# A 512-token Fourier mix inside a two-block kernel: one fold over tokens against two mirror folds with half the frequencies

## The reference, cut to what matters

```python
FOURIER_GROUPS, FOURIER_GROUP_DIM = 4, 128

def fourier_mix(f, w_f):          # f: (1, 512, 512)
    b, l, _ = f.shape
    fg = f.reshape(b, l, FOURIER_GROUPS, FOURIER_GROUP_DIM).astype(jnp.float32)
    z = jnp.fft.fft2(fg, axes=(1, 3), norm='ortho').real
    return z.reshape(b, l, FOURIER_WIDTH).astype(f.dtype) @ w_f

def merge_branches(h, ret_d, four_d, w_bg, b_bg, w_out):
    gates = jax.nn.sigmoid(h @ w_bg + b_bg)
    g_r, g_f = jnp.split(gates, N_BRANCHES, axis=-1)
    return (g_r * ret_d + g_f * four_d) @ w_out
```

## Time and profile before

| | us |
|---|---|
| median of 3 runs | 1664.74 |
| lowest and highest | 1662.05, 1671.71 |
| the profiled execution | 1659.04 |
| its span, first to last instruction | 1657.3 |
| mean granted TensorE clock, share of full | 0.983 |
| six steps with Fourier products, within the span | 1093.3 to 1146.8 |

### The profile page before, as it was taken

The page is one execution under the profiler, slowest core; times in us unless marked ns, Lnnn a source line. Parts: engine busy times, 40 slices in busy tenths (PEclk is TensorE's granted clock), DMA queues, the critical chain, the costliest instruction groups (busy, mean ns, idle before and its releaser), DMA issues.

```text
span 1657.3 us, 19932 instructions
## 1 busy us (share of the span) xinstructions
PE 1587.4 (96%) x7623; PEld 1273.9 (77%) x7623; DVE 895.6 (54%) x1071; ACT 772.0 (47%) x909; POOL 122.1 (7%) x95
## 2 busy tenths in 40 slices
PE   6999999999979899989799999999999999999998
PEld 5777777788867678878588888888887788888886
DVE  6424334345468788977453452523365655565464
ACT  5554445322457788855444333443124443443343
POOL 1101001000024233300010000000000000000000
PEclk9999999999979999999899999999999999999999
DMA  5457563234259999842412121321431333233222
GB/s 148 140 168 244 176 210 127 77 101 136 98 204 366 344 363 357 296 147 77 143 53 77 60 66 51 105 77 51 152 102 51 102 99 102 79 101 101 82 78 70
DMA packets 184033, 231.33 MB, mean 140 GB/s; under 512 B 14939, under 2 KB 155543, under 8 KB 180639
## 3 DMA queue, kind: packets, MB, share of 16 engines
q1 hardware_dynamic: 176223, 217.84, 39.9%
q0 software_dynamic: 7744, 12.60, 2.1%
HBM read 227.76 MB, written 18.37 MB: 149 GB/s over the span
## 4 chain that ended last, share of the span: by engine, by line
PE 85%; DMA 4%; DVE 4%; ACT 3%; issue 2%; SPq 1%; POOL 0%; ACTq 0%; POOLq 0%; DVEq 0%
PE psum L452 21%; PE psum L454 20%; PE psum L453 20%; DMA hg<-h_rows,at_row 3%; PE psum L1815 2%; PE psum L1816 2%; PE psum L1817 2%; PE psum L752 1%; PE psum L1791 1%; PE psum L834 1%; DMA vec<-in_ret_decay_b 1%; PE psum L1842 1%; DVE pre L531 1%; PE psum L1239 1%; PE psum L1843 1%
## 5 line engine op out<-in xcount | busy, mean ns | idle before, releaser
L452 PE MATMUL psum<-h_hi,w_hi 128*128 128x512 f32 x1160 | 462.9, 399 | 7.7 <-DVE w_lo L429 3.3
L454 PE MATMUL psum<-h_hi,w_lo 128*128 128x512 f32 x1160 | 453.1, 391 | 0.0
L453 PE MATMUL psum<-h_lo,w_hi 128*128 128x512 f32 x1160 | 453.0, 390 | 0.0
L429 DVE TENSOR_TENSOR w_lo<-raw,w_hi 128x2048 fp32r<-128x2048 f32 (+2 forms) x99 | 223.6, 2259 | 239.7 <-ACT w_hi L425 239.7
L452 PEld LDWEIGHTS psum<-h_hi,w_hi 128*128 128x128 f32 x1160 | 218.4, 188 | 67.7 <-issue 16.2
L454 PEld LDWEIGHTS psum<-h_hi,w_lo 128*128 128x128 f32 x1160 | 218.3, 188 | 46.9
L453 PEld LDWEIGHTS psum<-h_lo,w_hi 128*128 128x128 f32 x1160 | 218.6, 188 | 44.2 <-issue 1.4
L425 ACT ACTIVATE w_hi<-raw 128x2048 fp32r<-128x2048 f32 (+2 forms) x100 | 187.9, 1879 | 76.5 <-PE psum L454 68.8
L482 ACT ACTIVATE sq<-x 128x512 f32<-128x512 f32 x56 | 35.3, 632 | 151.8 <-DVE x L1352 105.2
L1761 DVE TENSOR_TENSOR w_lo_more<-raw_more,w_hi_more 128x2048 fp32r<-128x2048 f32 x34 | 77.8, 2287 | 20.3 <-ACT w_hi_more L1754 19.9
L1761 DVE TENSOR_TENSOR w_lo<-raw,w_hi 128x2048 fp32r<-128x2048 f32 x34 | 77.8, 2287 | 12.1 <-ACT w_hi L1754 11.7
(11 more groups left out here) (388 smaller groups left out, 2594.3 us busy)
## 6 DMA issues: line engine op xcount, KB each, us to landing
raw<-in_w_up SPq DMA_DIRECT2D x67, 512.0 KB, 8.2
wm_raw<-in_w_mod SPq DMA_DIRECT2D x24, 1024.0 KB, 5.5
raw<-in_w_in SPq DMA_DIRECT2D x18, 1024.0 KB
raw<-in_w_in SPq DMA_DIRECT2D x33, 512.0 KB
raw_more<-in_w_down SPq DMA_DIRECT2D x24, 512.0 KB, 5.4
raw<-in_w_gate SPq DMA_DIRECT2D x23, 512.0 KB, 5.4
raw_more<-in_w_gate SPq DMA_DIRECT2D x22, 512.0 KB, 5.3
raw_more<-in_w_up SPq DMA_DIRECT2D x22, 512.0 KB, 7.7
```

Of the source, the lines that this page charges most:

```text
L429: dve.tensor_tensor(w_lo[j][:, 0:tiles, :], raw[j][:, 0:tiles, :], w_hi[j][:, 0:tiles, :].bitcast(F32), ALU.subtract).then_inc(G["lo_ready ...
L452: pe.matmul(to, w_hi[j][:, tile, :], hi_k, start=(k == 0), stop=False)
L453: pe.matmul(to, w_hi[j][:, tile, :], lo_k, start=False, stop=False)
L454: return pe.matmul(to, w_lo[j][:, tile, :], hi_k, start=False, stop=last)
```

## The change

The token fold becomes a fold at two levels. Token t is paired with 512 - t: differences go to tokens 257 to 511, sums stay at 1 to 255; tokens 0 and 256 pair with themselves. Then sums are paired again around 128, and differences around 384. VectorE reads one operand of each pair backwards. Six instructions per group take the place of two. After this the four kinds of output (even and odd frequencies, cosine and sine part) each depend on one slice of 128 tokens, with one token left over (column 128 of the row).

Over features there are four products of 128 columns, cosines for the sums and sines for the differences, and one with a single column of weights, the left-over token, which goes to partition 0 of a second bank. ScalarE copies 512 columns and, in a second instruction, 128 columns of one partition. Over tokens there are five products: 129 columns that contract over one partition (the left-over token), then 129, 128, 127 and 128 columns, into one bank. Frequencies 0 to 256 come out as a cosine and a sine part.

ScalarE copies the sine part to `z_sin`; VectorE (`unfold`) writes two columns as they are and makes the others as sum and, for the mirrored frequencies, difference, with rows written in steps of 2 and -2, into `pre`. ScalarE waits for that and rounds `pre` into `z_hi`; VectorE makes `z_lo` from `pre`, now behind `yr_lo`. The table `dft_l` shrinks from 2048 to 641 columns per partition; the memory layout behind it is kept by padding.

```diff
--- before.py
+++ after.py
@@ -129,9 +129,11 @@
     j = np.arange(P)
     a = 2 * np.pi * np.outer(j, j) / P
     dft_d = np.concatenate([np.cos(a), -np.sin(a)], axis=1).astype(np.float32) / np.float32(256)
-    to = np.concatenate([t[0::2], t[1::2]])
-    a = 2 * np.pi * (np.outer(t[:T // 2], to) % T) / T
-    dft_l = np.stack([np.cos(a), np.sin(a)]).astype(np.float32)
+    j = np.arange(P + 1)
+    wave = lambda f, of, to: f(2 * np.pi * (np.outer(of, to) % T) / T)
+    dft_l = np.concatenate([wave(np.cos, j[:P], 2 * j), wave(np.cos, 127 - j[:P], 2 * j[:P] + 1),
+                            wave(np.sin, j[:P], 2 * j[1:P]), wave(np.sin, 128 - j[:P], 2 * j[:P] + 1),
+                            np.tile((-1.0) ** j, (P, 1))], axis=1).astype(np.float32)
     col, part = np.arange(P)[None, :], np.arange(P)[:, None]
     at = np.arange(1)[None, :]
 
@@ -379,7 +381,9 @@
                 yr_hi = buffers(r)("yr_hi", [P, KC, T], F32R)
             sb = buffers(s)
             z_room = sb("z_room", [P, NT * T])
-            dft_l = sb("dft_l", [P, 2, NT // 2, T])
+            dft_l = sb("dft_l", [P, T + P + 1])
+            z_sin = sb("z_sin", [P, 2, 2 * P])
+            z_pad = sb("z_pad", [P, 2 * T - P - 1])
             dft_d = sb("dft_d", [P, 2 * P])
             z_gap = sb("z_gap", [P, 1536])
             z_hi = sb("z_hi", [P, 4, T], F32R)
@@ -2545,8 +2549,7 @@
             sp.wait_ge(H["t_decayed"], 32)
             sp.wait_ge(H["t_vtok"], 8)
             sp.dma_start(dft_d[:, :], const["dft_d"]).then_inc(Z["z_const"], 16)
-            sp.dma_start(dft_l[:, :, :, :], const["dft_l"].rearrange("a (i p) t -> p a i t", p=P))\
-              .then_inc(Z["z_const"], 16)
+            sp.dma_start(dft_l[:, :], const["dft_l"]).then_inc(Z["z_const"], 16)
             for s in range(4):
                 load_slot(sp, G_GF + s, (G_GF + s) % 2, pairs(a["w_branch_gate_2"], D + s * 2 * P))
             for s in range(4):
@@ -2557,8 +2560,10 @@
                 load_slot(sp, G_FO + s, (G_FO + s) % 2,
                           [(0, 16, T, a["w_four_out_2"][:, s * T:(s + 1) * T].rearrange("(k p) n -> p k n", p=P))])
 
-        def in_order(g):
-            return psum[:, 5 + g % 2, :].rearrange("p (o j) -> p j o", o=2)
+        EVEN_C, ODD_C, EVEN_S, ODD_S, END = 0, P + 1, 2 * P + 1, 3 * P, 4 * P
+
+        def folded(g):
+            return fd[:, g, :, :].rearrange("p i n -> p (i n)")
 
         def four_tensor(pe):
             rest = ret_after_tensor(pe, 3)
@@ -2569,11 +2574,12 @@
                     pe.wait_ge(H["t_state"], 56)
                 else:
                     pe.wait_ge(Z["z_copied"], g)
-                pe.wait_ge(Z["z_fold"], 2 * g + 2)
-                for i in range(NT):
-                    done = pe.matmul(psum[:, SA + i // 2, (i % 2) * 256:(i % 2) * 256 + 256],
-                                     f_t[:, g, i * P:(i + 1) * P], dft_d[:, :], start=True, stop=True)
-                done.then_inc(Z["z_d"], 1)
+                pe.wait_ge(Z["z_fold"], 6 * g + 6)
+                for i, (t0, part) in enumerate(((0, 0), (P + 1, 0), (2 * P, 1), (3 * P, 1))):
+                    pe.matmul(psum[:, SA, i * P:(i + 1) * P], f_t[:, g, t0:t0 + P], dft_d[:, part * P:(part + 1) * P],
+                              start=True, stop=True)
+                pe.matmul(psum[0:1, SB, 0:P], f_t[:, g, P:P + 1], dft_d[:, 0:P], start=True, stop=True)\
+                  .then_inc(Z["z_d"], 1)
 
             def over_tokens(g):
                 pe.wait_ge(Z["z_copied"], g + 1)
@@ -2581,12 +2587,10 @@
                     pe.wait_ge(H["t_y"], 9)
                 if g >= 2:
                     pe.wait_ge(Z["z_lo"], g - 1)
-                for odd in range(2):
-                    cols = slice(odd * 2 * P, odd * 2 * P + 2 * P)
-                    for n in range(4):
-                        i, part = n // 2, n % 2
-                        done = pe.matmul(psum[:, 5 + g % 2, cols], fd[:, g, 2 * odd + i, part * P:(part + 1) * P],
-                                         dft_l[:, part, i, cols], start=(n == 0), stop=(n == 3))
+                to, of = psum[:, 5 + g % 2, :], folded(g)
+                pe.matmul(to[:, EVEN_C:ODD_C], of[0:1, 4 * P:5 * P], dft_l[0:1, END:END + P + 1], start=True, stop=False)
+                for i, (c0, c1) in enumerate(((EVEN_C, ODD_C), (ODD_C, EVEN_S), (EVEN_S, ODD_S), (ODD_S, END))):
+                    done = pe.matmul(to[:, c0:c1], of[:, i * P:(i + 1) * P], dft_l[:, c0:c1], start=(i > 0), stop=True)
                 done.then_inc(Z["z_l"], 1)
 
             for t in range(12):
@@ -2643,15 +2647,16 @@
                     rest[t]()
                 if 5 <= t < 9:
                     act.wait_ge(Z["z_d"], t - 4)
-                    act.activation(fd[:, t - 5, :, :], psum[:, SA:SA + 2, :].rearrange("p b (i n) -> p (b i) n", n=256),
-                                   ACT.Copy).then_inc(Z["z_copied"], 1)
+                    act.activation(folded(t - 5)[:, 0:4 * P], psum[:, SA, :], ACT.Copy)
+                    act.activation(folded(t - 5)[0:1, 4 * P:5 * P], psum[0:1, SB, 0:P], ACT.Copy).then_inc(Z["z_copied"], 1)
                 if t >= 5:
                     four_gate(act, t - 5)
                 if 7 <= t < 11:
                     g = t - 7
                     act.wait_ge(Z["z_l"], g + 1)
-                    act.activation(z_hi[:, g, :].rearrange("p (j o) -> p j o", o=2), in_order(g), ACT.Copy)\
-                       .then_inc(Z["z_hi"], 1)
+                    act.activation(z_sin[:, g % 2, 1:], psum[:, 5 + g % 2, EVEN_S:END], ACT.Copy).then_inc(Z["z_hi"], 1)
+                    act.wait_ge(Z["z_fold"], 6 * 4 + g + 1)
+                    act.activation(z_hi[:, g, :], pre[:, g % 2, :], ACT.Copy).then_inc(Z["z_hi"], 1)
                 if t >= 8:
                     gated_hi(t - 8)
             four_gate(act, 7)
@@ -2680,12 +2685,33 @@
                    .then_inc(Z["z_ylo"], 1)
 
             def fold(g):
-                early, late = f_t[:, g, 0:2 * P], f_t[:, g, 2 * P:4 * P]
+                n = 6 * g
+
+                f = f_t[:, g, :]
+                mirrored = ((f[:, 255:0:-1], f[:, 257:512]),
+                            (f[:, 127::-1], f[:, 129:257]),
+                            (f[:, 511:384:-1], f[:, 257:384]))
                 dve.wait_ge(Z["z_f"], g + 1)
-                dve.tensor_tensor(late, early, late, ALU.subtract).then_inc(Z["z_fold"], 1)
-                dve.wait_ge(Z["z_fold"], 2 * g + 1)
-                dve.scalar_tensor_tensor(out=early, in0=early, scalar=2.0, in1=late, op0=ALU.mult, op1=ALU.subtract)\
-                   .then_inc(Z["z_fold"], 1)
+                for level in (mirrored[:1], mirrored[1:]):
+                    for near, far in level:
+                        dve.tensor_tensor(far, near, far, ALU.subtract).then_inc(Z["z_fold"], 1)
+                    n += len(level)
+                    dve.wait_ge(Z["z_fold"], n)
+                    for near, far in level:
+                        dve.scalar_tensor_tensor(out=near, in0=near, scalar=2.0, in1=far, op0=ALU.mult, op1=ALU.subtract)\
+                           .then_inc(Z["z_fold"], 1)
+                    n += len(level)
+                    dve.wait_ge(Z["z_fold"], n)
+
+            def unfold(g):
+                dve.wait_ge(Z["z_hi"], 2 * g + 1)
+                at, z = psum[:, 5 + g % 2, :], pre[:, g % 2, :]
+                even_c, odd_c, even_s, odd_s = at[:, 1:P], at[:, ODD_C:EVEN_S], z_sin[:, g % 2, 1:P], z_sin[:, g % 2, P:]
+                dve.tensor_copy(z[:, 0:2 * P + 1:2 * P], at[:, 0:P + 1:P])
+                dve.tensor_tensor(z[:, 2:2 * P:2], even_c, even_s, ALU.add)
+                dve.tensor_tensor(z[:, T - 2:2 * P:-2], even_c, even_s, ALU.subtract)
+                dve.tensor_tensor(z[:, 1:2 * P:2], odd_c, odd_s, ALU.add)
+                dve.tensor_tensor(z[:, T - 1:2 * P:-2], odd_c, odd_s, ALU.subtract).then_inc(Z["z_fold"], 1)
 
             for t in range(12):
                 if t % 2 == 0:
@@ -2695,13 +2721,14 @@
                 if 2 <= t < 6:
                     fold(t - 2)
                 if 7 <= t < 11:
-                    g = t - 7
-                    dve.wait_ge(Z["z_hi"], g + 1)
-                    dve.tensor_tensor(z_lo[:, g, :].rearrange("p (j o) -> p j o", o=2), in_order(g),
-                                      z_hi[:, g, :].bitcast(F32).rearrange("p (j o) -> p j o", o=2), ALU.subtract)\
-                       .then_inc(Z["z_lo"], 1)
+                    unfold(t - 7)
                 if t >= 8:
                     gated_lo(t - 8)
+                if 7 <= t < 11:
+                    g = t - 7
+                    dve.wait_ge(Z["z_hi"], 2 * g + 2)
+                    dve.tensor_tensor(z_lo[:, g, :], pre[:, g % 2, :], z_hi[:, g, :].bitcast(F32), ALU.subtract)\
+                       .then_inc(Z["z_lo"], 1)
             for c in range(4, KC):
                 gated_lo(c)
             for c in range(KC):
```

## The result

The changed kernel took 1655.84 us (median of 16 runs, 1648.94 at the least), the kernel before 1663.88 (16 runs). One execution of each kernel was far slower than all others (1982.46 and 1788.88 us) and is left out of the ratio. The ratio of the means of the other 15 is 0.9942 with a 95% interval of [0.9925, 0.9958]: 9.6 us less, 0.58%. The forecast was 10.5 us less.

What follows compares the result with a forecast made beforehand. TensorE's queue was taken as the bound: 20.7 - 9.0 - 1.2 = 10.5 us off the profiled 1659.04 gives 1648.5, or 1654.2 against the median of 1664.74. The range was 1648 to 1660 us.

Steps and rivals of the forecast that it cites:

- What bounds the kernel: Steps with Fourier products: TensorE's queue sets the time; a microsecond less there is one less of the run.
- What goes and what comes: TensorE's Fourier products, four groups: 20.7 us go and 9.0 come, so the plain count saves 11.7 us.
- The narrow products: TensorE, left-over token: 0.3 us extra for the one-column product, 0 for the one-partition one; 1.2 us back over four groups.
- VectorE and ScalarE: Folds +4.6 and unfolds +5.3 us on VectorE, copies +1.6 us on ScalarE, all beside TensorE.
- Reversed and stepped rows: VectorE's unfold: from no cost to at most 0.6 us per unfold; none was taken.
- The handshake's cover: Even step of 7.7 us: ScalarE's and VectorE's work fits behind 24 weight products, about 6 us spare.
- Rival D: VectorE's unfold makes gates late and TensorE waits: decides above about 7 us; slower, 1673 us at 12; chance 0.02.
- A: TensorE's short products cost their whole load, 0.190 us a record: only 4.3 us off, 1660.4 us; chance 0.04.
- B: TensorE products with rows starting at an odd column stream slower: 1.1 us a group, 1658.7 us; chance 0.06.
- C: Narrow products stall TensorE 0.7 us each while the array empties: 5.6 us back, 1658.6 us; chance 0.09.

Runs made afterwards that it cites:

- before_half: The kernel before with four of its eight products over tokens left out; stretch 53.03 us against 59.94.
- no_left_over: The changed kernel without both products of the left-over token and its copy; stretch 46.36 us against 50.50.
- full_both: The changed kernel with both narrow products made full (128 weight columns; contraction over 128 partitions, table zero but for the first); stretch 48.19 us against 50.50.

## Why the prediction was right

**What bounds the kernel** was read rightly. Every microsecond taken from or put into TensorE's queue in this stretch showed in full: before_half took out 6.91 for 6.9, no_left_over 4.14 for 4.1, and behind the stretch lie 504.2 us in both, as in the kernels before and after (504.1 to 504.2). (full_both has 502.6 there. It lacks 3.4 us at a granted clock of 0.50 that the profile after shows at 1290.8 to 1294.2, so its span of 1652.0 flatters it by 1.6 us.)

**What goes and what comes** was right: 20.7 us out, 9.0 in, priced by L2191 and L2192. full_both has all ten products at 0.111 us a record and a stretch of 48.19, 11.75 us under before; the plain count said 11.7.

**The narrow products** are the term that was mis-sized. For the one-column product the 0.3 us taken from L2177's passage in and out was exact: 0.29 where it stands alone. For the one-partition product I took 0, after L2156; it costs 0.37 to 0.39 alone, more than the bound of 0.3 that I gave each product. Contracting over 64 partitions told nothing on contracting over one. With the shared passage in steps 7 and 8 the four groups pay 2.31 us, against the 1.2 that I put into the sum and the upper bound of 2.4 that I kept for the range. That the total stayed under 2.4 is luck: eight products alone would come to 4 x 0.29 + 4 x 0.38 = 2.7, and the shared passage was not foreseen. The 1.1 us between are the difference between the forecast of 10.5 and the stretch's 9.44. The lower bound, narrow products that run beside their neighbours, did not occur.

**VectorE and ScalarE** were costed too high, without effect: +7.6 and +0.5 us of busy time for +10 and +1.6, since short instructions that nothing separates overlap by 0.08 us each and the copy of one partition took 0.25, not 0.378. **Reversed and stepped rows** cost nothing. (Two slips without effect: the copy of `fd` ends at 2.9 us of the even step, not 2.8, and `dft_l` is 320.5 KB, which landed in 4.3 us, not 328.)

**The handshake's cover** was right in its verdict, no wait of TensorE, and wrong in its size. The step that failed is "about 6 us are spare": it looked at one step by itself, and a reduction of 4.41 us, inside those 6, made the stretch 2.95 us longer where it said none. Rival D was thus nearer than it was held to be: it decides at an unfold of some 4.6 us (0.9 plus the estimated 3.7), not 7, still five times the real one.

**The rivals.** A fell: 128-column products run at 0.111 to 0.114 us a record. The Trainium skill's page "TensorE: Matmul & The Clock Gate" has in its section "The mechanism" that a load overlaps running products only when their row groups differ, though the same section also lets a load into the background weight buffer go ahead. full_both, where all stand in the same row groups, shows the loads of 0.19 us overlapped with products 0.111 us apart, so the first sentence does not hold here. Its section "LDWEIGHTS (loading the stationary operand)", by which a load's time is its columns / 1.2 ns whatever the contraction, is borne out in direction only: a load of one column is a record of 80 ns, one of 128 columns 190, not 107, and one of 128 columns on a single partition 180. B fell: L2593 begins at odd columns and is not slower. Its price was also miscounted: three of the ten products, not five, start at column 129 or 257, which makes 0.7 us a group and not 1.1. C was right in place, passages around narrow products, and too high in price: 2.31 us in all, not 5.6.

**Against the chances**: the change is faster by 0.58%, interval 0.42 to 0.75%, so just on the side of "faster by over 0.5%" that had 0.73, with the line at 0.5% inside the interval.

## What to carry to other kernels

On a kernel whose TensorE queue has no gaps, price an edit by the distance between starts of the nearest product of the same type and width, and check it on a stretch between two fixed products: the stretch repeated to 0.02 us where whole runs scatter by 10. A product that is narrow in weights or in contraction (one column, one partition) is not small but a change of shape, 0.3 to 0.4 us here; padding it to the full array, or handing the rest to an idle vector engine, was faster. And when two helpers serve each other in every step, add their turns over all steps before calling anything spare.

## What the runs showed that I had not expected

Multiplying by zeros was the faster way: a full 128-partition contraction in place of one partition took 0.37 us off step 9. A one-partition product costs more than a one-column one (0.39 and 0.29 us above its 0.224), and the two side by side less than their sum (0.48 for 0.65). And at the routing, 600 us ahead of the change, the two profiles of either kernel part by 9 to 10 us, together with the granted clock: as much as the change is worth.
